# Order of scalar-engine work in a gate/up stage, a conditioning load in eight pieces, and one moved wait: one layer of a pooling and attention encoder

## The reference

```python
mod = (silu(c) @ w_ada + b_ada)                  # six rows of 1024: shift, scale, gate, twice
h = (layer_norm(x) * (1.0 + sc1) + sh1)
proj = h @ w_in                                  # pooling channels u, and q, k, v
mixed = concat(multiscale_pool(u), stick_breaking_attention(q, k, v))
x = layer_norm(ALPHA * x + g1 * (mixed @ w_o), ln1_g, ln1_b)
h = (layer_norm(x) * (1.0 + sc2) + sh2)
gu = h @ w_gu                                    # 1024 x 5632, gate half and up half
ff = (silu(gu[..., :2816]) * gu[..., 2816:]) @ w_down
x = layer_norm(ALPHA * x + g2 * ff, ln2_g, ln2_b)
```

## Time and profile before

| | |
|---|---|
| median of 3 runs | 2504.56 us (2501.0 to 2511.43) |
| the profiled execution | 2504.56 us, of which the profile's span is 2502.8 us |
| PE busy | 2388.5 us, 95% of the span |
| DVE, ACT, POOL busy | 58%, 42%, 35% |
| mean granted PE clock | 0.988 |

### The profile page before, as it was taken

How to read it: one execution, slowest core, us unless ns; L and a number is a source line. 1 busy time by engine, 2 the same in 40 slices (tenths; PEclk the granted TensorE clock), 3 DMA queues, 4 the chain that set the end, 5 groups by cost and what they waited for, 6 DMA issues and landing times.

```text
span 2502.8 us, 36208 instructions
## 1 busy us (share of the span) xinstructions
PE 2388.5 (95%) x14148; PEld 1324.8 (53%) x14148; DVE 1457.8 (58%) x1928; ACT 1039.9 (42%) x1629; POOL 881.5 (35%) x1032
## 2 busy tenths in 40 slices
PE   5999999899999889999999999999999999999998
PEld 3655555444444344555555553446666544788733
DVE  5757764788888887677788873324333211533214
ACT  2522332899999992234555542002222100233200
POOL 2300000577777671335467669001111420111100
PEclk8999999999999999999999999999999999999999
DMA  7215897333332113232565566744444446476555
GB/s 257 101 46 193 313 316 220 100 85 102 85 102 69 26 59 131 75 115 88 186 208 209 198 234 238 264 131 153 157 153 135 131 134 197 151 234 192 189 163 167
DMA packets 210148, 394.58 MB, mean 158 GB/s; under 512 B 30093, under 2 KB 142029, under 8 KB 201402
## 3 DMA queue, kind: packets, MB, share of 16 engines
q1 hardware_dynamic: 192986, 330.40, 40.1%
q10 hardware_dynamic: 16992, 61.87, 7.8%
HBM read 301.92 MB, written 90.30 MB: 157 GB/s over the span
## 4 chain that ended last, share of the span: by engine, by line
PE 68%; ACT 8%; POOL 7%; DVE 7%; DMA 5%; issue 4%; SPq 1%; ACTq 0%; POOLq 0%; DVEq 0%
PE ps L2757 22%; PE ps L2796 15%; PE ps L2348 11%; PE ps L2622 6%; DMA dn_dram<-work 3%; PE ps L2513 3%; PE ps L2497 3%; POOL work L1033 2%; PE ps L2474 2%; DVE work L1902 2%; ACT work L1292 2%; ACT ps L1303 2%; PE ps L2707 1%; ACT work L1380 1%; ACT work L1314 1%
## 5 line engine op out<-in xcount | busy, mean ns | idle before, releaser
L2757 PE MATMUL ps<-hidden_t,work 128*128 128x384 f16 (+1 forms) x4608 | 666.6, 307 | 6.6 <-issue 4.0
L2757 PEld LDWEIGHTS ps<-hidden_t,work 128*128 128x128 f16 x4608 | 449.6, 98 | 222.8 <-issue 10.1
L2796 PE MATMUL ps<-work 128*128 128x512 f16 x2244 | 473.8, 380 | 10.8 <-DVE work L2172 6.5
L2796 PEld LDWEIGHTS ps<-work 128*128 128x128 f16 x2244 | 206.1, 98 | 277.2 <-issue 32.3
L961 POOL TENSOR_TENSOR work<-work 128x512 f32<-128x512 f32 (+2 forms) x320 | 306.7, 962 | 125.2 <-DVE work L1902 70.3
L2348 PE MATMUL ps<-hidden_t,work 128*128 128x416 f16 (+2 forms) x1920 | 347.6, 339 | 1.4 <-DVE work L1736 0.6
L1033 POOL TENSOR_TENSOR work<-work 128x384 f16<-128x384 f32 (+1 forms) x116 | 117.8, 1022 | 506.9 <-ACT work L1469 506.9
L2348 PEld LDWEIGHTS ps<-hidden_t,work 128*128 128x128 f16 x1920 | 187.7, 98 | 149.1 <-issue 6.5
L1902 DVE TENSOR_TENSOR_SCAN work<-ps,work 128x512 f32<-128x512 f32 x192 | 237.2, 1270 | 18.5 <-ACT ps L1303 14.5
L908 POOL TENSOR_TENSOR work<-work,col 128x1 f32<-128x1 f32 x68 | 32.4, 476 | 501.7 <-DVE work L1624 501.6
L2189 DVE TENSOR_TENSOR work<-ps,work 128x1024 f32<-128x1024 f32 (+1 forms) x17 | 20.8, 1223 | 311.4 <-PE ps L2796 310.5
(11 more groups left out here) (268 smaller groups left out, 2887.6 us busy)
## 6 DMA issues: line engine op xcount, KB each, us to landing
work<-dn_dram ACTq DMA_DIRECT2D x96, 512.0 KB, 3.6
work<-gs_dram SPq DMA_DIRECT2D x88, 512.0 KB, 4.1
work<-gs_dram SPq DMA_DIRECT2D x44, 768.0 KB, 4.3
work<-in_w_gu SPq DMA_DIRECT2D x22, 1024.0 KB, 6.4
work<-in_w_gu SPq DMA_DIRECT2D x44, 512.0 KB, 5.0
gs_dram<-work SPq DMA_DIRECT2D x22, 1024.0 KB, 6.8
gs_dram<-work SPq DMA_DIRECT2D x66, 256.0 KB, 4.9
work<-in_w_ada SPq DMA_DIRECT2D x16, 1024.0 KB, 5.0
```

What stands on the lines that cost most here:

```text
L2757: mm = pe.matmul(ps[:, bank, 0:n], w, x, start=(q in (1, 2, 5) and k == 0 and (wh, xh) == (0, 0)), stop=(k == 3 and (wh, xh) == TERMS[-1]) ...
L2796: mm = pe.matmul(ps[r:r + rows, 2 * slot + half, :], E_HID[:, j, xh, at:at + rows], E_DHL[slab_home(g)][:, wh, 512 * half:512 * (half + 1) ...
```

## The change

Three places change, and no arithmetic does.

1. The `w_ada` load of the start is cut into eight transfers of 1 MB with rows of 1 KB, laid out so that each is one of PE's 256-column pieces. Two of them still count into one semaphore, and PE waits for both (32 instead of 16). The two `w_in` chunks may be queued after the first conditioning product instead of the second.
2. In the start, DVE does `low_a(0, 1)` ahead of its wait for the spread weight maxima and `low_a(0, 2)` ahead of `prep_low(0)`. PE's wait for `w_s` moves ahead of the 16 transposes of token group 1.
3. In stage E, group 0, ACT's list: `high_half(0, j, 1)` moves from the next slab (behind its `gu_split` and `copy2`) to the end of slab j, right behind `sigmoid2(j)`; `copy1(0, j+1)` moves from between the two pairs of `sum_split(j+1)` to behind the second pair, just ahead of `sigmoid2(j)`.

```diff
-        A_WADA = w32(6144, 16384).rearrange("p (s k n) -> p s k n", s=4, k=KD)
+        A_WADA = w32(6144, 16384).rearrange("p (s k n) -> p s k n", s=8, k=KD)
...
-                sp.dma_start(A_WADA[:, s, :, :], w_ada_k[:, :, 512 * s:512 * (s + 1)]).then_inc(wada_in[s], 16)
+                sp.dma_start(A_WADA[:, s, :, :], w_ada_k[:, :, 256 * s:256 * (s + 1)]).then_inc(wada_in[s // 2], 16)
...
-            for s in range(4):
+            for s in range(8):
                 load_ada(s)
-            sp.wait_ge(ada_mm, 2)
+            sp.wait_ge(ada_mm, 1)
...
                 if j > CUT:
-                    high_half(0, j - 1, 1)
                     high_half(0, j - 1, 0)
                 sigmoid1(0, j)
                 copy3(0, j)
                 if j + 1 < NF:
                     sum_split(j + 1, 0)
-                    copy1(0, j + 1)
...
                 if j + 1 < NF:
                     sum_split(j + 1, 1)
+                    copy1(0, j + 1)
...
                 sigmoid2(0, j)
-            high_half(0, NF - 1, 1)
+                high_half(0, j, 1)
             high_half(0, NF - 1, 0)
...
             top_of(ps[0:2, 2, 64:192], 2).then_inc(mod_max, 1)
+            low_a(0, 1)
             v.wait_ge(mod_ar, 4)
...
-            low_a(0, 1)
+            low_a(0, 2)
             prep_low(0)
-            low_a(0, 2)
             prep_low(1)
...
-                pe.wait_ge(wada_in[s // 2], 16)
+                pe.wait_ge(wada_in[s // 2], 32)
...
-                    pe.wait_ge(w_s, 2)
...
             pe.wait_ge(misc_in, 48)
+            pe.wait_ge(w_s, 2)
             for blk in range(3):
                 project_two(blk)
```

More of the change, by code:

```diff
@@ L2320, in _ @@
                     at = TS * (k % 4)
-                    mm = pe.matmul(ps[at:at + TS, 2 + s % 2, 256:512], CT[:, k, :], A_WADA[:, s // 2, k, 256 * (s % 2):256 * (s % 2 + 1)],
+                    mm = pe.matmul(ps[at:at + TS, 2 + s % 2, 256:512], CT[:, k, :], A_WADA[:, s, k, :],
                                    start=(k < 4), stop=(k >= 4))
```

## The result

The changed kernel takes 2519.04 us (median of 7 runs, 2515.26 to 2521.66) against 2504.56 (7 runs, 2501.0 to 2511.43): ratio 1.0053, 95% interval 1.0039 to 1.0067. So it is slower, by 10 to 17 us; I had forecast +10.8. The profiled execution took 2514.93 us, span 2513.2, the shortest of all, and its span is 10.4 us longer than the one of before. The medians lie 14.5 apart. Executions of one kernel differ by several us, so a small term can be read from single rows only where other executions with the same code show the same rows; where they don't, the text says so.

A forecast was written before the change was run, and what follows sets the result against it. PE, busy 95% of the span, was taken as the bound, except in gate/up, where a 14.1 us loop over POOL, ACT and DVE paces it. 2504.56 + 9.8 (loop) + 1.0 (start) = 2515.4 us, +0.43%; range 2504 to 2522.

The forecast's parts named there:

- The loop through POOL: Gate/up, group 0: ACT's new order lengthens the slab loop from 14.1 to 14.8 us, 14 intervals by 0.7, +9.8 us.
- the least: Lower bound for ACT's list in gate/up: 13 x 0.7 = 9.1 us, if the first interval still has cover.
- The exclusive port: DVE and POOL in gate/up: whichever begins first runs at own speed, the other stands still; POOL ends 0.77 behind gu_low.
- Steps 4 and 5: Gate/up slab: gu_low runs undisturbed in 2.34 us, ending at +7.8; POOL's second low part ends at +8.55 instead of +7.81.
- Step 4: Gate/up slab: gu_low waits for DVE, not gu_split; only 1.2 of 2.3 us count, so it begins at +5.45 instead of +4.23.
- the main pause ahead of product 1: Gate/up: PE can start its 48 matmuls at +7.9 instead of +7.14, behind gu_low, with intervals of 14.8 us.
- The pause of 0.2 to 0.3 us ahead of product 6: Gate/up: PE waits for copy1, done at +1.13; a second small pause of 0.2 to 0.3 us that costs nothing further.
- The load: Start, w_ada in eight pieces: nothing comes sooner, 1 KB rows run at 386 against 388 GB/s, price 0.0 to 0.1 us.
- my bound of 0.8: Start, upper bound for the w_ada load's cost: a loss of 5% on 6.3 MB, 0.8 us.
- The start's waits: Start: DVE's order and PE's wait leave PE idle 2.05 us instead of 0.57; whole start +1.0 us, between 0.7 and 3.3.
- the clock still rising where it did: Start: if the clock still rises at 58.1, 1.5 us more idling at half speed is 0.75 us at full.
- The further stretch of 3.4 us at half speed: Start: if the clock's rise moves with the work plus one such stretch, the cost is 0.75 + 1.7 = 2.5 us.

The follow-up runs named there:

- ff_only: Kernel before with only ACT's two moves in gate/up of group 0 (high_half and copy1): ratio 1.0049 (1.0033 to 1.0064).
- high_only: Kernel before with only high_half(0, j, 1) moved behind sigmoid2: 14.60 us a slab, where the kernel before has 14.10.
- pool_after: Changed kernel with POOL's first two weight differences of the next slab moved ahead of its two low parts: ratio 0.9978 to the kernel before, 13.65 us a slab.
- copy_only: Kernel before with only copy1(0, j+1) moved behind the second pair of sum_split: 14.50 us a slab, where the kernel before has 14.10.
- load_only: Kernel before with only the w_ada load in eight 1 MB transfers of 1 KB rows and w_in queued earlier: third piece pair at 33.32 us, 31.82 before.
- dve_only: Kernel before with only DVE's new order in the start: 5.18 us from the spread maxima to the projection, 4.76 before.
- load_2k8: Kernel before with the w_ada load in eight 1 MB transfers cut along row blocks, keeping 2 KB rows: third piece pair at 31.90 us, 31.82 before.

## Why the prediction came out as it did

- **The loop through POOL, +9.8 us predicted.** Right in mechanism and nearly in size: 9.05 us, since the period is 14.78 and not 14.80, and the first interval costs 0.1 and not 0.7. I had named 9.1 as the least for this reason. ff_only, high_only and pool_after show the cause.
- **The exclusive port.** Steps 4 and 5 rested on it, and gu_low takes 2.35 and POOL ends 0.77 behind it, as read. What the Trainium skill (SBUF — State Buffer, "SBUF: two separate sides") says of the exclusive lock agrees with copy_only as well: there POOL's low part begins 0.01 us ahead of gu_low and keeps its 0.91, and gu_low takes 3.06.
- **What releases gu_low.** Step 4 is right that gu_low does not wait for gu_split, but I had missed that it is held by POOL's first low part, which follows gu_split. In the changed kernel this makes no difference; in copy_only it is why 14.50 came out and not 14.30.
- **Where PE stops.** Wrong: I put the main pause ahead of product 1 and took the products behind product 6 to be covered. PE stops for copy2 ahead of product 7 instead, 0.54 us, and copy2 stands behind the late gu_split on ACT. I had overlooked that product 7 waits for copy2. Product 7 ends at the same time as gu_low, so no time hangs on it. The pause of 0.2 to 0.3 us ahead of product 6 came as foreseen.
- **The load, +0.0 to 0.1 us predicted.** This is the term that was mis-sized, and the sign that I gave for it failed (33.59 instead of 31.8): 1.5 us in load_only, 1.8 in the changed kernel, and past my bound of 0.8. I took the rate of 1 KB rows from one window of 1 us of a single 1 MB transfer, 386 GB/s, with a DMA share of 1.08 beside 1.05. In a long stream the rows give 348; why the short one reaches 386 was not tried. The estimate from the Trainium skill (DMA: Bandwidth & Descriptors, "Why small descriptors are slow (HBM only)") was 4.5%; the trace disagrees, 348 being 10% under 388.
- **The start's waits.** PE idles the 2 us foreseen. 1.2 us of delay come from it where I had 1.5, and 0.76 are left behind the faster first matmuls, against 0.9 (1.0 less the load's 0.1). This is the case that I had priced as the clock still rising where it did: it rises at 58.1 in the kernel before, 1 us into the first 12 matmuls, and at 60.3 in the changed one (windows in the last section), as they begin. So it moved by 2.2 us, about as the spread maxima did, while the matmuls moved by 3.17. That it came out so is in part luck, since in dve_only the clock reads 0.50 until about 62.3. The further stretch of 3.4 us at half speed, which the upper end of the range allows for, no run shows as such; what they show is the 2.1 us by which the 4.88 of dve_only are above 2.75.
- **Not foreseen, -2.0 us.** I had written that a move of other stages by more than a microsecond would speak against the prediction. The first down pass did move, but runs without any change in gate/up or down show waits between 3.2 and 6.5 us there. The 2.0 us belong to the two executions compared, not to the change.

Sum by rows: 2.7 (start) + 9.05 (slabs) + 0.7 (last slab and start of down) - 2.0 = 10.4 us, the difference of the spans. The last slab's 0.4 is in ff_only too; the 0.3 at the start of down is within what unchanged kernels show (1.15 to 1.63 us of wait there). Without the 2.0 the rows give 12.4, nearer to the 14.5 of the medians, whose interval holds both. The forecast of +10.8 is near the foot of that interval: its main term is right, it lacks the load's 1.5 us, and that it all but meets the 10.4 of the profiled pair is luck. What the medians have beyond the rows stays unassigned.

## What to carry to other kernels

Before moving an instruction on a helper engine, write down the loop that releases the matrix engine, with the time of each step from one zero, and see which engine waits inside it: here the gain was not in reordering the engine that looked busy but in giving POOL's 4 us of waiting two instructions that need nothing. Where two engines exclude each other, the one that comes second is tied to whatever releases the first, and a move can change which of them leads, so moves don't add up. A stage in which nothing was changed must be compared over several executions before a difference in it is given to the change. Take a transfer rate from a stream as long as the one to be changed, and read it together with the busy share.

## What the runs showed of the hardware

PE's pace and the granted clock that the profile shows are not always the same thing in the start. This window of the changed kernel lies within the 16 transposes that start at 39.14 and take 3.65 us, and reads a granted clock of 1.00 (columns as in the earlier trace rows):

```profile
39.20:42.40 3.20, 3.20 (x17) 3.19 (x16) 0.00 (x0) 0.00 (x0) 0.00 (x0) 1.00 1.01 233
```

In the kernel before the same 16 transposes took the same 3.65 us at a clock of 0.50:

```profile
37.40:41.00 3.60, 3.60 (x21) 3.27 (x24) 0.00 (x0) 0.00 (x0) 0.00 (x0) 0.50 0.70 156
```

At 77.59, in the changed kernel, 16 such transposes take 1.91 us, so at 39.14 PE ran at about half pace with 1.00 shown as granted. Which of the two, the clock shown or something else that slows PE, is the cause, no run here tells. Around 60.3 us, where the first 12 matmuls of the projection begin, the two agree; the 16 transposes ahead of it take 3.59 us and the 8 behind it 1.04:

```profile
57.00:60.30 3.30, 3.30 (x16) 3.25 (x17) 2.51 (x3) 3.30 (x4) 1.32 (x1) 0.50 0.43 175
60.30:62.90 2.60, 2.60 (x15) 1.23 (x13) 2.60 (x3) 2.60 (x5) 0.96 (x1) 1.00 0.00 0
```

A slow stretch can thus not be read off the granted clock alone; the length of like instructions has to be put beside it.

The rate of this load, 8 MB in a stream, went with the length of its rows: 346 to 350 GB/s with rows of 1 KB (load_only) and 383 to 390 with rows of 2 KB (load_2k8), with 8 transfers of 1 MB each time.
